# Heads stage of a gated linear attention block: GpSimd in place of VectorE makes the rests of 15 gate weight units, and the state products are issued as column halves

## The reference, cut to what matters

```python
f = lbf + (1.0 - lbf) * jax.nn.sigmoid(f_logit.astype(f32))
k, logf = 1.0 - f, jnp.log(f)
def step(S, inp):
    q_, k_, v_, a_ = inp
    o_inter = jnp.einsum('bhtk,bhkv->bhtv', q_ * jnp.exp(a_), S)
    decay = jnp.exp(jnp.where(causal, a_[..., :, None, :] - a_[..., None, :, :], -jnp.inf))
    scores = jnp.einsum('bhtsk,bhsk->bhts', q_[:, :, :, None, :] * decay, k_)
    o = o_inter + jnp.einsum('bhts,bhsv->bhtv', scores, v_)
    S = jnp.exp(a_last)[..., None] * S + jnp.einsum('bhsk,bhsv->bhkv', k_ * jnp.exp(a_last - a_), v_)
    return S, o
...
mix = jax.nn.sigmoid(ga) * (o_a @ w_branch_a[l]) + jax.nn.sigmoid(gb) * (o_b @ w_branch_b[l])
```

## Time and profile before

| | |
|---|---|
| median of 3 runs | 1996.39 us (1995.15 to 1996.77) |
| the profiled execution's own time | 1996.64 us |
| its span in the trace | 1994.9 us |
| TensorE (PE) | 1970.6 us busy, 99% of the span |
| VectorE (DVE) | 1092.7 us busy, 55% |
| ScalarE (ACT) | 853.5 us busy, 43% |
| GpSimd (POOL) | 201.4 us busy, 10% |

### The profile page before, as it was taken

The page is one execution under the profiler, slowest core; times in us unless marked ns, Lnnn a source line. Parts: engine busy times, 40 slices in busy tenths (PEclk is TensorE's granted clock), DMA queues, the critical chain, the costliest instruction groups (busy, mean ns, idle before and its releaser), DMA issues.

```text
span 1994.9 us, 31378 instructions
## 1 busy us (share of the span) xinstructions
PE 1970.6 (99%) x11631; PEld 1727.1 (87%) x11631; DVE 1092.7 (55%) x1878; ACT 853.5 (43%) x1274; POOL 201.4 (10%) x195
## 2 busy tenths in 40 slices
PE   8999999999999999999999999999999999999998
PEld 7989989999888988889988888888889888888887
DVE  6235999555653566577654433444656654433443
ACT  6224665543223554466643222234666543212333
POOL 2004111200100110001001100110014001100100
PEclk9999999999999999999999999999999999999999
DMA  4322111233333324331033332332332133323332
GB/s 140 110 83 78 53 54 54 78 92 95 90 102 107 95 84 115 107 96 42 12 95 95 99 102 84 95 110 79 103 87 65 43 95 95 108 82 95 95 101 79
DMA packets 320578, 174.21 MB, mean 87 GB/s; under 512 B 5216, under 2 KB 317920, under 8 KB 320496
## 3 DMA queue, kind: packets, MB, share of 16 engines
q1 hardware_dynamic: 320496, 173.11, 29.7%
HBM read 170.99 MB, written 2.10 MB: 87 GB/s over the span
## 4 chain that ended last, share of the span: by engine, by line
PE 95%; DVE 3%; issue 1%; ACT 1%; DMA 0%; SPq 0%; POOL 0%; POOLq 0%; DVEq 0%; ACTq 0%
PE ps L2194 54%; PE ps L2200 27%; PE ps L2812 3%; PE ps L2772 2%; PE ps L2797 2%; PE ps L2347 1%; PE ps L2408 1%; PE ps L2750 1%; PE ps L2751 1%; PE ps L2687 1%; PE ps L2441 0%; DVE w_lo L1385 0%; PE ps L2822 0%; DMA x_rows<-x 0%; PE ps L2299 0%
## 5 line engine op out<-in xcount | busy, mean ns | idle before, releaser
L2194 PE MATMUL ps<-z_hi,w_hi 128*128 128x512 f32 (+2 forms) x2032 | 623.6, 345 | 0.0
L1385 DVE TENSOR_TENSOR w_lo<-raw,w_hi 128x1024 fp32r<-128x1024 f32 (+2 forms) x298 | 385.9, 1295 | 430.3 <-ACT w_hi L829 429.0
L2194 PE MATMUL ps<-z_lo,w_hi 128*128 128x512 f32 (+2 forms) x2032 | 614.8, 341 | 0.0
L829 ACT ACTIVATE w_hi<-raw 128x1024 fp32r<-128x1024 f32 (+2 forms) x298 | 328.3, 1102 | 443.1 <-PE ps L2200 408.0
L2200 PE MATMUL ps<-z_hi,w_lo 128*128 128x512 f32 (+2 forms) x2032 | 433.0, 341 | 0.0
L2194 PEld LDWEIGHTS ps<-z_hi,w_hi 128*128 128x128 f32 x2032 | 352.0, 189 | 50.9 <-issue 3.1
L2194 PEld LDWEIGHTS ps<-z_lo,w_hi 128*128 128x128 f32 x2032 | 350.8, 189 | 44.7
L2200 PEld LDWEIGHTS ps<-z_hi,w_lo 128*128 128x128 f32 x2032 | 333.3, 189 | 45.2
L2194 PE MATMUL ps<-g_hi,w_hi 128*128 128x512 f32 (+1 forms) x539 | 209.4, 390 | 0.0
L2194 PE MATMUL ps<-g_lo,w_hi 128*128 128x512 f32 (+1 forms) x539 | 208.8, 389 | 0.0
L760 POOL TENSOR_TENSOR g_lo<-gv,g_hi 128x512 f32 x65 | 84.4, 1299 | 1062.5 <-ACT g_hi L1240 1062.5
(11 more groups left out here) (352 smaller groups left out, 2413.3 us busy)
## 6 DMA issues: line engine op xcount, KB each, us to landing
raw<-w_gate_up SPq DMA_DIRECT2D x88, 512.0 KB, 3.9
raw<-w_down SPq DMA_DIRECT2D x48, 704.0 KB, 4.8
raw<-w_in SPq DMA_DIRECT2D x44, 512.0 KB, 3.9
raw<-w_up SPq DMA_DIRECT2D x44, 512.0 KB, 3.8
raw<-w_out SPq DMA_DIRECT2D x24, 512.0 KB, 4.0
raw<-w_in_b SPq DMA_DIRECT2D x14, 512.0 KB, 3.8
raw<-w_in_a SPq DMA_DIRECT2D x12, 512.0 KB, 3.8
raw<-w_branch SPq DMA_DIRECT2D x8, 512.0 KB, 3.9
```

The lines of the kernel that those rows point to most:

```text
L829: act.activation(w_hi[s][:, 0:width], raw[s][:, 0:width], ACT.Copy).then_inc(hi_done, 1)
L1385: dve.tensor_tensor(w_lo[s][:, 0:width], raw[s][:, 0:width], w_hi[s][:, 0:width].bitcast(F32), ALU.subtract).then_inc(lo_done, 1)
L2194: pe.matmul(out, w_hi[s][:, w0 + k * P:w0 + (k + 1) * P], rhs[:, lo:lo + width], start=a, stop=False)
```

## The change

VectorE's two rests of a head leave its list; GpSimd makes them (15 units: all gate units from n+2 on, and the unit n+16 that follows them). TensorE writes each state product as two matmuls of 64 weight columns.

```diff
+            def gate_lo(n, s):
+                pool.wait_ge(hi_done, n + 1)
+                pool.wait_ge(lo_done, n + 2)
+                pool.tensor_tensor(w_lo[s][:, 0:UNIT], raw[s][:, 0:UNIT], w_hi[s][:, 0:UNIT].bitcast(F32),
+                                   ALU.subtract).then_inc(lo_done, 1)
             def head(h):
+                n = UNITS["gates"]
+                if h:
+                    gate_lo(n + 2 * h + 1, 1)
                 pool.wait_ge(mx["o"], h + 1)
                 pool.tensor_copy(vh[:, :, :], V[:, :, h * VD:(h + 1) * VD]).then_inc(mx["vh"], 1)
                 pool.tensor_copy(vh0[:, :], V0[:, h * VD:(h + 1) * VD]).then_inc(mx["vh"], 1)
                 pool.wait_ge(mx["qe_exp"], 2 * h + 1)
                 pool.tensor_tensor(qe[:, :], qe[:, :], qf[:, 2 * h, META:], ALU.mult).then_inc(mx["qe"], 1)
+                gate_lo(n + 2 * h + 2, 0)
...
                 mul_right(0)
                 mul_right(1)
-                if h:
-                    split_lo(n + 2 * h + 1, 1)
...
                 mul_right(3)
-                split_lo(n + 2 * h + 2, 0)
                 take(h, 2)
...
             scaled_pair(2)
+            dve.wait_ge(lo_done, n + 19)
             split_lo(n + 17, 1)
...
+            def column_halves(out, weights, moving, start, stop):
+                for t in range(2):
+                    x = pe.matmul(out[t * VD:(t + 1) * VD], weights[:, t * VD:(t + 1) * VD], moving, start=start, stop=stop)
+                return x
...
                 for c in range(4):
                     lhs = kdt[0:META, 0, :] if c == 0 else kdt[:, c, :]
                     rhs = vh0[:, :] if c == 0 else vh[:, c - 1, :]
-                    x = pe.matmul(ps[2][:, 0, c * VD:(c + 1) * VD], lhs, rhs, start=True, stop=True)
+                    x = column_halves(ps[2][:, 0, c * VD:(c + 1) * VD], lhs, rhs, True, True)
                 x.then_inc(mx["turn"], 1)
```

## The result

The changed kernel took 2006.37 us (median of six executions, 2005.88 to 2009.15), the kernel before 1995.83 us (six, 1995.15 to 1996.77). The ratio is 1.0055 with a 95% interval of 1.0043 to 1.0068: slower, by 10.5 us, where 10.2 were forecast. The profiled execution took 2005.88 us with a span of 2004.1 us, 9.2 us over the span before.

What follows compares the result with a forecast made beforehand. TensorE and VectorE bound the heads stage in turn. Gains -7.5, VectorE held by GpSimd +14.7 and clock falls +3.0 make +10.2 us on 1996.4: 2006.6 us, forecast range 1999.5 to 2012, 8 in 10 from 1994 to 2016.

Steps and rivals of the forecast that it cites:

- The two segments: Each head: TensorE sets the pace from `outputs` to the states (12.6 us), VectorE from the states to `outputs` (6.9 us).
- rest A: Unit n+2h+1's rest, on GpSimd between states and `outputs`: holds VectorE 2.1 us in seven heads, +14.7 us.
- rest B: Unit n+2h+2's rest, on GpSimd ahead of the states' sums: VectorE's 0.94 us wait covers the hold, cost 0.
- GpSimd's rest: One rest on GpSimd takes 2.4 us and holds VectorE's operations that read two SBUF tensors for 2.2 us.
- What the hold costs: VectorE's segment before `outputs` has nothing to spare, so 2.1 us in each of seven heads: +14.7 us.
- The states: State products as sixteen matmuls take the diagonal's 0.63 us, not 1.24: 0.6 us less in 8 heads, -4.9 us.
- rival 4: The column halves do nothing for the states: +15.1 us, about 2011.5 us; chance counted within the forecast's 0.58.
- The rests off VectorE: Taking rest A off VectorE shortens TensorE's stops ahead of levels 1 and 2: 2.9 us saved over the heads.
- The clock: Stops of about 2.1 us ahead of `outputs` drop TensorE's clock in two heads of seven, 1.5 us each: +3.0 us.
- Rival 1: GpSimd waits until VectorE stops, so `outputs` starts on time: no change, about 1996 us; chance 0.15.
- Rival 2: Port given back within GpSimd's long operation, VectorE loses under 0.3 us per rest A: about 1991 us; chance 0.12.
- Rival 3: The clock falls in every head with a rest A: +19.1 us, about 2015.5 us; chance 0.15.

Runs made afterwards that it cites:

- rest B alone: Against the changed kernel: rest B (unit n+2h+2) stays on GpSimd, rest A returns to VectorE, column halves kept; 1993.97 us, ratio 0.9988.
- rest A alone: Against the changed kernel: rest A (unit n+2h+1) stays on GpSimd, rest B returns to VectorE, column halves kept; 2004.71 us, ratio 1.0048.
- the memset: Against the changed kernel: GpSimd fills the rests' buffer with zeros, reading nothing and leaving 15 rests uncomputed; 1989.46 us, ratio 0.9966.
- the halves alone: Against the kernel before: state products as two matmuls of 64 weight columns, nothing moved to GpSimd; 1993.22 us, ratio 0.9986.

## Why the prediction was right

The time was 0.2 us from the forecast, which is more luck than the terms deserve. The terms as measured are -7.2 (both gains), +12.6 (seven stops), +3.0 (two falls), -1.7 (a fall that went) and +1.2 (mostly in heads 5 and 6, below): 7.9 us, where the profiled executions differ by 9.2 and the medians by 10.5. Of the 1.3 us between 7.9 and 9.2, 0.4 were there before the first rest (head 0's `qe` starts at 190.30 and 190.72 us); the rest I can't place. The medians differ by more than the profiled executions, and the forecast left out or misjudged terms both ways that nearly cancel.

**The two segments: right.** `outputs` waits for `take(h, 6)` and has a stop in each of the seven heads with a rest A and in no other kernel but those with a reading GpSimd there. The same hold in the segment of TensorE (rest B alone) costs 0.75 us, in that of VectorE (rest A alone) 11.5 us.

**GpSimd's rest: right.** 2.4 us estimated, 2.39 to 2.54 measured. The hold is 2.08 us where 2.1 was taken. That is close by two small errors: rest A is 2.50 us long, 0.1 more than estimated, and `sub` was issued 0.28 us behind GpSimd's start, which the 2.2 us for the gap didn't count. By the Trainium skill ("SBUF — State Buffer", section "Who interferes with whom") the second to issue is blocked for the whole instruction, so `sub` would have begun at GpSimd's recorded end, 252.10 us; the trace has 249.88 + 2.50 - 0.42 = 251.96, 0.14 us earlier.

**What the hold costs: mis-sized a little.** I multiplied 2.1 us by seven, since VectorE had "nothing to spare" ahead of `take`. It had a little: the stops are 1.80 us, 12.6 in all, and not 14.7. With rest B alone, `take(2, 6)` was done 0.30 us ahead of `outputs` (246.91 and 247.21 us), and in the changed kernel 0.11 us ahead.

**The states: mis-sized.** I gave sixteen matmuls the diagonal's 0.63 us; they take 0.83, so 0.4 us a head and 3.2 us in all, not 4.9. The direction was right, and rival 4 is out. The view of the weight loads shows where the 0.4 us are, before and after:

```profile
260.21 1.10 PEld L2441 LDWEIGHTS ps<-vh,kdt 16*128 16x128 f32 x8
...
265.74 0.69 PEld L2196 LDWEIGHTS ps<-vh,kdt 16*64 16x64 f32 x16
```

Eight loads of 128 columns take 1.10 us and sixteen of 64 take 0.69, so 0.41 less. The Trainium skill's load time by columns ("TensorE: Matmul & The Clock Gate", section on LDWEIGHTS) gives an estimate of 0.85 us for the sixteen loads and the same for the eight. The trace agrees with neither, and as a rule of what splitting does, the measurement contradicts it. Why halves of the same total columns load faster than wholes stays open.

**The rests off VectorE: mis-sized the other way.** Put at 2.9 us, measured at 4.0 with the memset. Together with the halves that is 7.2 us, where I had taken 7.5; the two errors cancel, by luck.

**The clock: a guess that one execution matches, and an incomplete count.** Two falls of 1.5 us came in the stage in the profiled execution; the other five had lower clocks, so the number is luck. I hadn't seen that the fall behind it could go, which gives 1.7 us back. Set against the memset kernel, in which `outputs` never waits and no fall is in this stretch, the difference closes: over heads 1 to 6 the stretches add up to 130.16 us in the changed kernel and to 116.66 with the memset (119.25 with the halves alone). Of the 13.5 us between them six stops make 10.8 and one fall 1.5. Of the 1.2 left 1.1 are in heads 5 (0.3) and 6 (0.8): in head 5 TensorE stands 0.35 us ahead of level 2, in head 6 the 0.56 us ahead of the states, and beside the memset it does neither. The second is rest B's, as it is there with rest B alone too (0.54 us). So its "Cost 0", read from head 3, doesn't hold in every head.

**The rivals.** Rival 1 (GpSimd kept out until VectorE stops) has a true mechanism in the wrong place. GpSimd is kept out between back-to-back operations of VectorE, as in the earlier trace rows; where rest A asks, it gets in at the end of `less_decay`. What the two places differ in is that `sub(h, 0)` waits for a semaphore of `less_decay`, with 0.03 us between the two; that this gap is what lets GpSimd in fits the rows shown here, but was only argued. Forced, its course costs 1998.8 us and not 1996, because the forecast had left out `vh` and `qe` behind it. Rival 2 (the port released within) is out: hold and operation shrink together. Rival 3 (a fall in every head) didn't come, but the kernel with whole states, whose stops are 0.1 us longer, had four of them for seven stops in its profiled execution. My term for the clock was a guess with bounds and not a derivation.

## What to carry to other kernels

Before giving an "idle" GpSimd a two-input operation of VectorE's, find the segment in which it will run. In this kernel a reading GpSimd held VectorE's two-input work (and the `tensor_scalar` `kk`) for nearly the length of its own operation, 2.08 us of 2.50, so it was free only where VectorE waits for something else or works from PSUM, and cost nearly its length where the next engine waited for VectorE. Here 2.4 us on GpSimd replaced 1.14 us on VectorE, so even with nothing paid for it there were only 4.0 us of 1996 to win; the same kind of rest cost about nothing in one segment and 11.5 us in the other. And moving such an operation elsewhere in a list moves all that is queued behind it: price those too.

## What was not expected of the hardware

- A stop of TensorE between 1.6 and 1.9 us costs the clock in some places and not in others. In the profiled executions, of seven stops of 1.80 us two were followed by 3.4 us at 1.2 GHz in the changed kernel and one with rest A alone; of seven of 1.92 us four were. With rest A behind `take(h-1, 6)` the stop of 1.75 us in head 6 had a fall and the one of 1.77 in head 4 none; two stops of 1.62 us had none. The one of 1.86 us behind the stage had a fall before the change and none after, and none with the halves alone either. What decides stays open.
- A GpSimd operation that asks first isn't always let in first. Asked for at 249.92 us, rest A began by my estimate (3.55 us less its usual 2.5) at about 251.0, near the end of the second `mul_right` (251.23 us), which VectorE had issued after it.
- Sixteen float32 matmuls with 64 weight columns take 0.83 us where eight with 128 take 1.24, for the same product; the weight loads alone go from 1.10 to 0.69 us.
